# A two-layer decoder step on one core: the key-value and mid-state products of the retention layer from hi and lo parts, and the states moved by GpSimd

## The reference

```python
def retention_chunk(q, k, v, s_prev, log_gamma):
    ...
    scores = jnp.einsum('bhnd,bhmd->bhnm', q, k) * decay_mask[None].astype(q.dtype)
    inner = jnp.einsum('bhnm,bhme->bhne', scores, v)
    cross = jnp.einsum('bhnd,bhde->bhne', q, s_prev.astype(q.dtype)) * cross_decay[None, :, :, None].astype(q.dtype)
    kv = jnp.einsum('bhmd,bhme->bhde', k * k_decay[None, :, :, None].astype(k.dtype), v)
    s_new = jnp.exp(log_gamma * L)[None, :, None, None] * s_prev + kv
    return inner + cross, s_new.astype(s_prev.dtype)
...
def retention_mixer(h, pos, s0, w_in, w_out, lead):
    ...
    of = o.astype(jnp.float32)
    mu = jnp.mean(of, axis=-1, keepdims=True)
    var = jnp.mean(jnp.square(of - mu), axis=-1, keepdims=True)
    o = ((of - mu) * lax.rsqrt(var + GN_EPS)).astype(h.dtype)
    return (jax.nn.silu(g) * o) @ w_out, s
```

## Time and profile before

| | us |
|---|---|
| median of 3 runs (1456.8 to 1457.08) | 1457.04 |
| the profiled execution | 1458.02 |
| its span in the profile | 1454.7 |
| TensorE busy | 1449.2 |
| VectorE busy | 799.9 |
| ScalarE busy | 543.2 |

### The profile page before, as it was taken

The page is one execution under the profiler, slowest core; times in us unless marked ns, Lnnn a source line. Parts: engine busy times, 40 slices in busy tenths (PEclk is TensorE's granted clock), DMA queues, the critical chain, the costliest instruction groups (busy, mean ns, idle before and its releaser), DMA issues.

```text
span 1454.7 us, 27349 instructions
## 1 busy us (share of the span) xinstructions
PE 1449.2 (100%) x11428; PEld 1395.2 (96%) x11428; DVE 799.9 (55%) x1066; ACT 543.2 (37%) x776; POOL 2.9 (0%) x24
## 2 busy tenths in 40 slices
PE   9999999999999999999999999999999999999998
PEld 9699789879979999999999999999999999999998
DVE  7885577468458855555542427444565555553222
ACT  5552273264155543333331314222343333332222
POOL 0000000000000000000000000000000000000000
PEclk9999999999999999999999999999999999999999
DMA  8445253463444322222222222232223222222221
GB/s 302 149 186 192 96 225 107 180 232 104 166 162 178 115 89 87 89 98 87 87 93 100 87 88 88 88 97 92 89 89 100 87 87 99 88 87 101 92 88 59
DMA packets 47742, 171.94 MB, mean 118 GB/s; under 512 B 5608, under 2 KB 6248, under 8 KB 46624
## 3 DMA queue, kind: packets, MB, share of 16 engines
q1 hardware_dynamic: 47488, 170.76, 33.8%
q0 software_dynamic: 32, 0.03, 0.0%
q10 hardware_dynamic: 144, 0.00, 0.0%
HBM read 149.44 MB, written 21.55 MB: 118 GB/s over the span
## 4 chain that ended last, share of the span: by engine, by line
issue 100%; POOL 0%; POOLq 0%
POOLq L107 0%; POOL ident L266 0%; POOL h_tail L263 0%; POOL k_tail_stack L275 0%; POOL mean_v L259 0%; POOL ident L257 0%; POOL h_hi L261 0%; POOL h_lo L262 0%; POOL sample_ones L274 0%; POOL sample_ones L279 0%; POOL mean_d L258 0%; POOL late_q_decayed L276 0%; POOL seed L268 0%; POOL seed L269 0%; POOL seed L271 0%
## 5 line engine op out<-in xcount | busy, mean ns | idle before, releaser
L846 ACT ACTIVATE w_hi<-w_raw 128x1024 fp32r<-128x1024 f32 x227 | 240.1, 1059 | 671.4 <-PE ps L405 469.1
L405 PE MATMUL ps<-h_hi,w_hi 128*128 128x264 f32 (+2 forms) x2300 | 468.3, 285 | 0.4 <-DVE h_lo L1184 0.4
L405 PE MATMUL ps<-h_lo,w_hi 128*128 128x264 f32 (+2 forms) x2300 | 465.4, 284 | 0.0
L405 PE MATMUL ps<-h_hi,w_lo 128*128 128x264 f32 (+2 forms) x2300 | 464.9, 283 | 0.0
L1159 DVE TENSOR_TENSOR w_lo<-w_raw,w_hi 128x1024 fp32r<-128x1024 f32 x227 | 277.0, 1222 | 334.5 <-ACT w_hi L846 334.2
L405 PEld LDWEIGHTS ps<-h_hi,w_hi 128*128 128x128 f32 x2300 | 355.8, 188 | 1.5 <-issue 0.8
L405 PEld LDWEIGHTS ps<-h_hi,w_lo 128*128 128x128 f32 x2300 | 355.5, 188 | 0.0
L405 PEld LDWEIGHTS ps<-h_lo,w_hi 128*128 128x128 f32 x2300 | 355.3, 188 | 0.0
L695 PE MATMUL ps<-z_hi,w_lo 128*128 128x264 f32 (+1 forms) x704 | 144.7, 283 | 0.0
L695 PE MATMUL ps<-z_lo,w_hi 128*128 128x264 f32 (+1 forms) x704 | 144.6, 283 | 0.0
L695 PE MATMUL ps<-z_hi,w_hi 128*128 128x264 f32 (+1 forms) x704 | 144.6, 283 | 0.0
(11 more groups left out here) (205 smaller groups left out, 1407.7 us busy)
## 6 DMA issues: line engine op xcount, KB each, us to landing
w_raw<-in_w_units_dram SPq DMA_DIRECT2D x227, 512.0 KB, 3.3
states<-in_state_ret_dram SPq DMA_DIRECT2D x32, 512.0 KB, 8.5
out_ret_s_dram<-states SPq DMA_DIRECT2D x32, 512.0 KB, 4.6
v_bcast<-v_scratch SPq DMA_DIRECT2D x8, 1024.0 KB, 5.6
x_res<-in_x_all_dram SPq DMA_DIRECT2D x8, 268.0 KB, 6.0
out_ret_p_dram<-tmp SPq DMA_DIRECT2D x4, 512.0 KB, 3.7
out_y_prompt_dram<-y_rows SPq DMA_DIRECT2D x4, 512.0 KB, 2.6
decay<-in_decay_dram SPq DMA_DIRECT2D x4, 299.5 KB, 3.8
```

Of the source, the lines that this page charges most:

```text
L405: out = mm(PS[:, 2 * s + half, at:at + n_col], a, b[:, lo:lo + n_col], start=first and n == 0, stop=last and n == 2)
L846: fn(WH[:, c % NS, :], RAW[:, c % NR, :], ACT.Copy).then_inc(hi_ready, 1)
```

## The change

- Keys and values are split into float32r parts (`KNH`, `KNL`; `VH`, `VL`), and so are the mid state (`KMH`, `KML`) and the late queries (`QLH`, `QLL`). Each of the eight 512-column products of L573 and the eight 280-column products of L602 of a head becomes three float32r products. The inner products of the scores stay float32.
- ScalarE drains all four value blocks, each twice (`V`, `VH`); VectorE forms the rests. VectorE drains none.
- On TensorE the score part of the inner products of dt = 0 comes ahead of the second half of the key-value sums, which alternate with its mid-state products.
- `outer` and `update` go from the inner stage to the output projection: in heads 0 to 2 after p = 1 (states 0, 1), p = 2 (2, 3) and p = 3 (4 to 7); in head 3 after p = 0 and p = 1, the last four in the first body of the ConvFFN. On ScalarE they stand ahead of the norm of the pair's tiles, on VectorE behind it.
- GpSimd issues the loads and stores of the states, the key-value output and the broadcast of the sample values, the last after the inner products, since `v_bcast` now lies over `V`, `PR` and `VS`. SP issues weights and the decay table, and takes the next head's units 0 to 3 at the end of a head.
- `KV` lies in `G`; the last sum of the key-value output takes a second instruction. ScalarE's wait for the last stores goes into the first ConvFFN body.

```diff
+UPDATES = (((), (0, 1), (2, 3), (4, 5, 6, 7)), ((0, 1), (2, 3), (), ()))
...
+with ExitStack() as s8:
+    KMH = sb("mid_state_hi", [P, 2 * DV], F32R, scope=s8)
+    KML = sb("mid_state_lo", [P, 2 * DV], F32R, scope=s8)
...
+        VH = sb("v_rows_hi", [P, 4, DV], F32R, scope=s3)
...
+    VB = sb("v_bcast", [P, NB, DV], scope=s2)
...
+    with ExitStack() as s7:
+        KNH = sb("k_rows_hi", [P, 4, DK], F32R, scope=s7)
+        KNL = sb("k_rows_lo", [P, 4, DK], F32R, scope=s7)
...
+    def state_stream(h):
+        def broadcast():
+            for half in range(2):
+                b = half * NB // 2
+                pool.dma_start(VB[:, b:b + NB // 2, :], VSCR[b:b + NB // 2, :].partition_broadcast(P)).then_inc(vb_in[half], 16)
+        for b in range(NB):
+            if h > 0:
+                pool.wait_ge(s_out[b], 16 * h)
+            elif b == 0:
+                pool.wait_ge(ss_sum, 7)
+            pool.dma_start(S[:, b, :], st_in[b, h]).then_inc(s_in[b], 16)
+        pool.wait_ge(v_tail, 4 * h + 4)
+        pool.dma_start(VSCR, V[16:24, 4, :]).then_inc(v_sent, 16)
+        pool.wait_ge(kv_ready, h + 1)
+        pool.dma_start(kv_dst[h], KV).then_inc(kv_sent, 16)
+        pool.wait_ge(v_sent, 16 * h + 16)
+        pool.wait_ge(inner_done, 4 * h + 4)
+        broadcast()
+        for b in range(NB):
+            pool.wait_ge(s_upd, NB * h + (b + 1))
+            pool.dma_start(st_out[b, h], S[:, b, :]).then_inc(s_out[b], 16)
+    for h in range(HEADS):
+        state_stream(h)
...
+    def head(h, first, last):
+        for n in range(4, 6):
             in_heads(h, n)
         if first:
             sp.wait_ge(ss_sum, 7)
         else:
             sp.wait_ge(s_upd, NB * h)
         sp.dma_start(DEC[:], io["decay"][h]).then_inc(dec_in, 16)
...
+        for n in range(6, 16):
             in_heads(h, n)
...
+        for n in range(4):
+            next_unit(h, n)
...
+            if j < 3:
+                pe.wait_ge(v_hi, 4 * h + (1, 3, 4)[j])
             for e in range(2):
...
+        def key_value(e, js):
+            for j in js:
+                kh, kl = KNH[:, j, e * P:(e + 1) * P], KNL[:, j, e * P:(e + 1) * P]
+                for q, (k, v) in enumerate(((kh, VH), (kh, VL), (kl, VH))):
+                    out = mm(PS[:, 6 + e, :], k, v[:, j, :], start=j in (0, 2) and q == 0, stop=j == 1 and q == 2)
+            return out
+        for e in range(2):
+            pe.wait_ge(kn_lo, 4 * h + 2 * e + 2)
+            pe.wait_ge(v_lo, 4 * h + 4)
+            key_value(e, (0, 1)).then_inc(mid_done, 1)
+        def key_value_end(e):
+            pe.wait_ge(mid_lo, 2 * h + e + 1)
+            key_value(e, (2, 3))
+            pe.wait_ge(kt_hi, 2 * h + 2)
+            pe.wait_ge(kt_lo, h + 1)
+            pe.wait_ge(vs_hi, 2 * h + 2)
+            pe.wait_ge(vs_lo, h + 1)
+            return mm(PS[:, 6 + e, :], KT[0:96, e * P:(e + 1) * P], VS[0:96, :], start=False, stop=True)
+        def early_values(dt):
             for j in range(2):
...
+                mm(PS[:, 2 * INNER[dt], CUT + q0:2 * CUT], V[0:mn, j, dt * P:(dt + 1) * P],
...
+        def mid_queries(dt, e):
+            pe.wait_ge(ql_lo, 2 * h + e + 1)
+            pe.wait_ge(mid_lo, 2 * h + e + 1)
+            km = slice(e * DV + dt * P, e * DV + (dt + 1) * P)
+            for q, (k, c) in enumerate(((KMH, QLH), (KMH, QLL), (KML, QLH))):
+                mm(PS[:, 2 * INNER[dt] + 1, 0:N_LATE + NB], k[:, km], c[:, e, :], start=e == 0 and q == 0, stop=False)
+        def late_values(dt):
+            at = 2 * INNER[dt] + 1
+            for j in range(2, 4):
+                mm(PS[:, at, BLK[j][0] - CUT:TP - CUT], V[:, j, dt * P:(dt + 1) * P], PR[:, PCOL[j]:PCOL[j + 1]], start=False, stop=False)
+            return mm(PS[:, at, 4 * P - CUT:T - CUT], VS[:, dt * P:(dt + 1) * P], SS[:], start=False, stop=True)
+        pe.wait_ge(p_ready, 5 * h + 5)
+        pe.wait_ge(ss_hi, 2 * h + 2)
+        pe.wait_ge(const_ready, QL_ZERO)
+        pe.wait_ge(ss_lo, h + 1)
+        early_values(0)
+        key_value_end(0)
+        mid_queries(0, 0)
+        key_value_end(1).then_inc(kv_done, 1)
+        mid_queries(0, 1)
+        late_values(0).then_inc(inner_done, 1)
+        for dt in range(1, 4):
+            if dt == 2:
+                pe.wait_ge(kv_sum, h + 1)
+            if dt == 3:
+                pe.wait_ge(o_ready, 4 * h + 1)
+            early_values(dt)
             for e in range(2):
...
+                mid_queries(dt, e)
+            late_values(dt).then_inc(inner_done, 1)
...
+    def outer(h, b):
+        if b == 0:
+            act.wait_ge(z_mul, 8 * h + 8)
+        if b in (0, NB // 2):
+            act.wait_ge(vb_in[b // (NB // 2)], 16 * h + 16)
+        if b >= 2:
+            act.wait_ge(s_upd, 8 * h + (b - 1))
+        for e in range(2):
+            at = (b % 2) * 1024 + e * DV
+            fn(G[:, at:at + DV], VB[:, b, :], ACT.Copy, scale=KD8[:, e, b:b + 1]).then_inc(samp_kv, 1)
     def head(h, first, last):
...
+        for b in range(4):
+            if b < 3:
+                act.wait_ge(v_acc, 3 * h + b + 1)
+            else:
+                act.wait_ge(unit_done, U_HEAD * h + (NS + 8))
             fn(V[:, b, :], PS[:, 2 + b, :], ACT.Copy, scale=RN[:, b:b + 1]).then_inc(v_ready, 1)
...
+            fn(VH[:, b, :], PS[:, 2 + b, :], ACT.Copy, scale=RN[:, b:b + 1]).then_inc(v_hi, 1)
...
+        if first:
+            act.wait_ge(prep_step, 12)
...
         for j in range(4):
...
+            fn(KNH[:, j, :], src, ACT.Copy, scale=DEC[:, DEC_ROW + j:DEC_ROW + j + 1]).then_inc(kn_ready, 1)
...
+        def mid_hi(e):
+            act.wait_ge(mid_done, 2 * h + e + 1)
+            fn(KMH[:, e * DV:(e + 1) * DV], PS[:, 6 + e, :], ACT.Copy).then_inc(mid_ready, 1)
+        mid_hi(0)
+        for e in range(2):
+            act.wait_ge(ql_ready, 2 * h + e + 1)
+            fn(QLH[:, e, 0:N_LATE], QT[:, e, :], ACT.Copy).then_inc(ql_hi, 1)
+        mid_hi(1)
         split_hi(5 + NS, U_HEAD, h)
...
         split_hi(6 + NS, U_HEAD, h)
...
         split_hi(7 + NS, U_HEAD, h)
...
                 split_hi(12 + p + NS, U_HEAD, h)
+            for b in UPDATES[last][p]:
+                outer(h, b)
             if last:
                 for k in (2 * p, 2 * p + 1):
                     act.wait_ge(x_written, XW_RET - 8 + k + 1)
                     norm_tile(k, 1, C_RET, N_RET, D_FFN)
...
                 root(3, n_in // 2, halves(R[:, c0:]), rstd)
+            if first and l == 0:
+                for b in range(4, NB):
+                    outer(HEADS - 1, b)
...
+    def update(h, b):
+        dve.wait_ge(samp_kv, 16 * h + (2 * b + 2))
+        at = (b % 2) * 1024
+        stt(S[:, b, :], S[:, b, :], DEC[:, DEC_STATE:DEC_STATE + 1], G[:, at:at + 1024], ALU.mult, ALU.add).then_inc(s_upd, 1)
...
+        for b in range(4):
+            dve.wait_ge(v_ready, 5 * h + b + 2)
+            dve.wait_ge(v_hi, 4 * h + b + 1)
+            tt(VL[:, b, :], V[:, b, :], VH[:, b, :].bitcast(F32), ALU.subtract).then_inc(v_lo, 1)
+            if b < 2:
+                dve.wait_ge(v_tail, 4 * h + 4)
+                tt(QT[:, b, :], Q[:, b, CUT:TP], DEC[:, DEC_Q:DEC_ROW], ALU.mult).then_inc(ql_ready, 1)
+        def k_rest(j):
+            if j % 2 == 0:
+                dve.wait_ge(kn_ready, 4 * h + j + 2)
+            src = PS[:, 6 + j // 2, (j % 2) * DK:(j % 2 + 1) * DK]
+            stt(KNL[:, j, :], src, DEC[:, DEC_ROW + j:DEC_ROW + j + 1], KNH[:, j, :].bitcast(F32),
+                ALU.mult, ALU.subtract).then_inc(kn_lo, 1)
+        k_rest(0)
+        k_rest(1)
...
+        k_rest(2)
+        k_rest(3)
...
+        def mid_rest(e):
+            dve.wait_ge(mid_ready, 2 * h + e + 1)
+            mid = slice(e * DV, (e + 1) * DV)
+            tt(KML[:, mid], PS[:, 6 + e, :], KMH[:, mid].bitcast(F32), ALU.subtract).then_inc(mid_lo, 1)
+        mid_rest(0)
         dve.wait_ge(ss_hi, 2 * h + 2)
         tt(SS[32:56, :], SE[0:24, :], SS[0:24, :].bitcast(F32), ALU.subtract).then_inc(ss_lo, 1)
...
+        for e in range(2):
+            dve.wait_ge(ql_hi, 2 * h + e + 1)
+            tt(QLL[:, e, 0:N_LATE], QT[:, e, :], QLH[:, e, 0:N_LATE].bitcast(F32), ALU.subtract).then_inc(ql_lo, 1)
+        mid_rest(1)
+        split_lo(NS + 5, U_HEAD, h)
+        split_lo(NS + 6, U_HEAD, h)
...
+        tt(KV, PS[:, 6:8, :].rearrange("p e v -> p (e v)"), KMH[:].bitcast(F32), ALU.add).then_inc(kv_sum, 1)
+        dve.wait_ge(kv_sum, h + 1)
+        tt(KV, KV, KML[:].bitcast(F32), ALU.add).then_inc(kv_ready, 1)
+        split_lo(NS + 7, U_HEAD, h)
...
-        dve.wait_ge(s_upd, NB * h + NB)
+        dve.wait_ge(kv_sent, 16 * h + 16)
...
                     norm_tile(k, 1, C_RET, N_RET, D_FFN)
+            for b in UPDATES[last][p]:
+                update(h, b)
...
                 dve.wait_ge(r_ready, norm_no + 1)
+                if l == 0:
+                    for b in range(4, NB):
+                        update(HEADS - 1, b)
```

(35 more changed lines are left out.)

108 lines of the change are left out of this document (23 added, 85 removed).

## The result

| | before | changed |
|---|---|---|
| median, us | 1457.04 | 1460.66 |
| ratio, 95% interval | | 1.0024 (1.0016 to 1.0032) |
| profiled execution, us | 1458.02 | 1460.94 |
| its span, us | 1454.7 | 1459.2 |

The forecast was 1456.1; the time is 3.6 us above the kernel before and 0.2 above the end of the range, which reached to 1460.5. The page of the changed kernel, against the earlier trace rows: TensorE is busy for 5.3 us less in a span that is 4.5 us longer.

A forecast was written before the change was run, and what follows sets the result against it. TensorE, busy 1449.2 of 1454.7 us, was taken as the bound. Products -8.0, waits in heads +2.5, ConvFFN entry +4.5 sum to -1.0 us: 1457.04 to 1456.1 us, range 1450 to 1460.5, likeliest case 1454.1 to 1459.9.

The forecast's parts named there:

- Moved: the transfers: State loads and stores on GpSimd's queue, weights on SP: no engine waits for them, issue taken as 0.7 us, cost nothing.
- the two waits: TensorE's new waits inside the heads, 2.5 us (bounds 0.5 and 4), and entering the ConvFFN, 4.5 us (bounds 3 and 6).
- a late state: State transfers through GpSimd reaching the next head late: 1.5 us allowed in the range's upper end.
- Gain of the products: Key-value and mid-state products on TensorE as float32r: 2.0 us less a head, 8.0 us in all.
- The 11.5: Alternative gain on TensorE by the four-pass rule for true FP32: 2.9 us a head; the prediction took 8.0 instead.
- Wait for `ss_lo`: TensorE waits in each head for VectorE's `ss_lo`: 1.1 us in head 0, 0.45 in the others, 2.5 in sum.
- Entry: Entry into the ConvFFN after head 3: four updates between norm tiles make TensorE late by 4.5 us, paid once.
- The fallen clock, named as a risk: TensorE's clock falling after a gap, listed among things that would make the forecast wrong; no size given.
- Other covers: Heads 0 to 2's updates, first ConvFFN body's reads and inner-slot copies stay hidden: cost nothing; body covered by 3 us.
- Rival 1: Waits in heads and at the ConvFFN are hidden: 1449.0 us, or 1451.3 with half the latter; chance 0.27 with the four-pass rule.
- rival 3: Float32r products of these operands take no less than float32 ones on TensorE: 1464.1 us; chance 0.02.
- Rival 2: GpSimd's issues make states late: 1463.6 us at 2.0 us per issue; chance 0.13, shared with entry wait beyond 7 us.

The follow-up runs named there:

- the run whose clock held: Changed kernel with 48 transfers of 8 bytes added to GpSimd's queue at 511 us, ahead of the sample output; 47.55 us from statistic to statistic, drain 6.20 us.

## Why the prediction was wrong, and where it was right

**The step that failed** is "Moved: the transfers", with its "Cost nothing". It followed every issue of GpSimd's queue to who waits for its data, and found rightly that nobody is late: the issues take 0.51 to 0.68 us, less than the 0.7 taken, the state loads 9.1 us to land, and no engine waited for a state. It did not ask what stands behind the last instruction of that queue. The sum was made up to the end of TensorE's work, and the 4.63 us from its last group (1450.05) to the end of the span were carried over as they were. What the runs showed in its place: the drain that comes with that instruction grew from 2.44 to 7.25 us, the span now ends 9.30 us behind TensorE's last group, and giving that one transfer to SP brought 4.9 us back. The profile of before had the hint: its chain of waits ends on GpSimd's queue, with the sample output, though the bound is TensorE. Whatever makes this queue's end dearer is paid in full. No row priced it, since the queue had carried one transfer; but the step could have named the end as an unknown cost, as it did with the issue. That the time lies only 0.2 us above the range is chance: the range's upper end adds bounds of the two waits and a late state, none of which was reached, and the drain is not among its terms.

**The forecast of the rest held.** Without the drain on the path the changed kernel takes 1455.78 us; 1456.1 was forecast. By the terms below it would be 1457.04 - 7.6 + 2.5 + 4.3 = 1456.2; the rest is smaller than what the start alone makes, which differs by up to 0.85 us, and the kernel before gained 0.3 us with the same edit, within its noise. That the sum is this close is partly chance, and the terms are the better test:

- Gain of the products: 8.0 forecast. Their starts lie (187.19 - 184.88) / 10 = 0.231 us apart with 512 columns and (190.51 - 190.25) / 2 = 0.13 with 280, as taken; without the wait for `ss_lo` a head takes 15.00 us for 16.96, which is 1.96 a head, and 1.72 in head 0, where 0.24 goes to the wait for the mid state's rest: 7.6. The 11.5 that the prediction worked out from the four passes of the Trainium skill (FP8 and Floating Point Precision, TensorE Precision Notes), each at the price of a float32r product, did not come: a product that three float32r products replace here cost 0.86 / 0.231 = 3.7 of them. Whether it takes four passes that are each shorter, no run tells.
- Wait for `ss_lo`: 1.1 and 3 x 0.45 forecast, 0.92 and 3 x 0.54 by the run without it, 2.5 in both sums. The end of `ss_lo` came at 187.76; the forecast's 188.1, less the 0.4 us that this head starts earlier, is 187.7.
- Entry: 4.5 forecast, 4.32 measured. VectorE came as forecast: the adds of p = 1 end at 482.34, those of p = 2 at 489.82, the last tile sum at 497.90; with the 4.65 us by which the gate statistic stands earlier than before, that is 486.99, 494.47 and 502.55, where 487.0, 494.5 and 502.5 were forecast. The gaps of 1.9, 1.7 and 0.7 are 1.84, 1.30 and 0.49 in the run whose clock held. In the changed kernel the second gap is missing: at half clock TensorE needs 489.97 - 482.49 = 7.48 us for the products of p = 3, 1.65 more than 5.83, and comes 0.15 us after the adds have ended (488.51 + 1.31). The fallen clock, named as a risk, cost nothing, because VectorE sets the time of the norm statistic.
- Other covers (updates in heads 0 to 2, the first body's reads, the copies for the inner slots): no wait of TensorE names them, and the stretch from the norm statistic to the last group is 0.13 us longer.

**The rivals.** Rival 1 (waits hidden) and rival 3 (products no cheaper) fell with the rows above. Rival 2 came out on the right side, for a wrong reason: it had GpSimd's queue as the place, the issue as the price, and late states as the way. The rule behind it, from the Trainium skill (SBUF — State Buffer, Who interferes with whom), is not contradicted, but no stall shows: all 81 issues lie between 0.51 and 0.68 us. The chance for slower was 0.15.

## What to carry to other kernels

GpSimd's queue had a cost at its end here, and not only at each issue. Before transfers are moved to another engine, look at what the last instruction of that engine is and whether the program's end waits for it; the last step of the chain of waits tells, even where another engine is busy for 100%. Where a queue has carried dozens of transfers on GpSimd, let its last one come early and give the final store to another queue: here one moved instruction was worth 4.9 us. And an engine that is idle for half of the span can still be the bound where its work is dense: the updates cost 4.3 us between the norm tiles and nothing 10 us earlier or later.

## What the runs showed of the hardware

- The drain at the end of GpSimd's queue takes 3.75 us after 33 transfers, 7.2 to 7.7 after 80 or 81 and 9.90 after 113, of 8 bytes or of 512 KB; 6.20 after 129 and 3.59 after 161, unexplained.
- In the changed kernel TensorE's granted clock, at 1.00 (2.4 GHz) ahead of it, was 0.53 over the 3.3 us from 483.3 (nearly all of it at 1.2 GHz) after an idle time of 1.86 us that ended at 482.49, and was back at 1.00 by 487. With the same gap of 1.84 to 1.86 us in the same place it fell in the profiled executions of the changed kernel and of the runs with the sample output on SP and with the later wait for `ss_lo`, and stayed at 1.00 in those of the runs with one pair of updates and with 48 more transfers. It is not the kernel that decides: with the sample output on SP it fell in the profiled execution and, by their mean clock of 1.000, not in three others. What does decide it stays open.
- Behind the first float32r product of 512 columns after float32 ones the next product starts 0.34 us later (184.54 to 184.88 in head 1), behind the following ones 0.23 us later.
